# Seven-product blocks: running sums in two PSUM banks, four ScalarE copies and one 512-column VectorE addition instead of one copy and five additions

## The reference

```python
def hybrid_layer(x, ...):
    h = rms_norm(x, norm1_g)
    q, k, v, iq, ik, iw, a, c, g = split(h @ w_in, IN_SPLITS)
    # sparse attention on q, k, v, iq, ik, iw; convolutions on a and c
    ...
    # gated outputs of the three branches, the product with w_o, and a
    # feed-forward part (w_up, a short convolution, w_down)
```

## Time and profile before

| | |
|---|---|
| time, median of 3 runs | 1971.0 us (1969.97 to 1972.1) |
| span of the profiled execution | 1967.1 us |
| median of the runs less that span | 3.9 us |
| PE busy | 1954.6 us, 99% of the span |
| PEld busy | 1848.6 us, 94% |
| DVE busy | 1194.6 us, 61% |
| POOL busy | 1119.2 us, 57% |
| ACT busy | 402.2 us, 20% |

### The profile page before, as it was taken

How to read it: one execution, slowest core, us unless ns; L and a number is a source line. 1 busy time by engine, 2 the same in 40 slices (tenths; PEclk the granted TensorE clock), 3 DMA queues, 4 the chain that set the end, 5 groups by cost and what they waited for, 6 DMA issues and landing times. The chain is left out here.

```text
span 1967.1 us, 37363 instructions
## 1 busy us (share of the span) xinstructions
PE 1954.6 (99%) x14834; PEld 1848.6 (94%) x14834; DVE 1194.6 (61%) x3033; ACT 402.2 (20%) x978; POOL 1119.2 (57%) x750
## 2 busy tenths in 40 slices
PE   9999999999999999999999999999999999999999
PEld 7788889999899999999999899999999999999998
DVE  4244535989978477524888987667713487554541
ACT  2241521111321222110111222222102025220000
POOL 1000038785176588758678155487776674448783
PEclk9999999999999999999999999999999999999999
DMA  5313445444444454445444343454444442445544
GB/s 212 134 43 132 150 151 179 160 164 139 149 144 143 156 174 167 171 148 172 168 159 168 121 162 131 150 172 172 167 164 161 136 147 97 140 150 172 172 161 140
DMA packets 44267, 299.76 MB, mean 152 GB/s; under 512 B 5440, under 2 KB 6592, under 8 KB 10176
## 3 DMA queue, kind: packets, MB, share of 16 engines
q1 hardware_dynamic: 42560, 295.42, 43.7%
q10 hardware_dynamic: 1536, 1.97, 0.3%
HBM read 294.35 MB, written 1.05 MB: 150 GB/s over the span
## 5 line engine op out<-in xcount | busy, mean ns | idle before, releaser
L712 PE MATMUL bank<-arena,ring 128*128 128x128 f32 (+2 forms) x3854 | 603.4, 310 | 1.2 <-ACT arena L1344 0.6
L712 PEld LDWEIGHTS bank<-arena,ring 128*128 128x128 f32 x3854 | 540.4, 191 | 43.6 <-ACT arena L1344 3.1
L712 PE MATMUL bank<-xn,ring 128*128 128x128 f32 (+3 forms) x3104 | 467.8, 306 | 0.0
L712 PEld LDWEIGHTS bank<-xn,ring 128*128 128x128 f32 (+1 forms) x3104 | 424.4, 191 | 31.1 <-issue 4.4
L712 PE MATMUL bank<-arena 128*128 128x128 f32 (+3 forms) x3048 | 391.5, 284 | 0.0
L712 PEld LDWEIGHTS bank<-arena 128*128 128x128 f32 (+1 forms) x3048 | 364.9, 192 | 9.3 <-issue 1.5
L712 PE MATMUL bank<-arena,h_res 128*128 128x128 f32 x2696 | 322.4, 276 | 2.1 <-POOL h_res L1802 1.2
L712 PEld LDWEIGHTS bank<-arena,h_res 128*128 128x128 f32 x2696 | 310.6, 192 | 5.1 <-POOL h_res L1802 2.4
L1798 POOL TENSOR_TENSOR arena<-ring 128x1024 f32<-128x1024 f32 (+1 forms) x103 | 243.0, 2360 | 124.7 <-DMA ring<-wstream 124.2
L1798 POOL TENSOR_TENSOR h_res<-ring 128x1024 f32<-128x1024 f32 (+1 forms) x95 | 221.7, 2334 | 127.1 <-DMA ring<-wstream 111.9
L1849 DVE SCALAR_TENSOR_TENSOR bank<-arena,par,bank 128x256 f32<-128x256 f32 x640 | 259.5, 483 | 15.3 <-DVE arena L2265 7.7
(11 more groups left out here) (241 smaller groups left out, 1805.0 us busy)
## 6 DMA issues: line engine op xcount, KB each, us to landing
ring<-wstream SPq DMA_DIRECT2D x264, 1024.0 KB, 4.8
ring<-wstream SPq DMA_DIRECT2D x16, 768.0 KB, 4.2
cst<-consts SPq DMA_DIRECT2D x1, 2488.0 KB, 14.7
h_res<-tokens SPq DMA_DIRECT2D x2, 544.0 KB, 5.1
arena<-arena ACTq DMA_DIRECT2D x16, 64.0 KB, 3.4
out<-arena SPq DMA_DIRECT2D x4, 256.0 KB, 5.4
arena<-arena ACTq DMA_DIRECT2D x28, 32.0 KB, 3.1
ring<-wstream SPq DMA_DIRECT2D x2, 288.0 KB, 2.9
```

The lines of the kernel that those rows point to most:

```text
L712: return pe.matmul(o, lhs, rhs, start=start, stop=stop, skip_group_check=True)
```

## The change

The 179 fast blocks other than `down` and the first `attn` become `chain_block`. Products now add up in PSUM: P6 onto P1 and P7 onto both, P3 onto P5. Since a partial sum is wanted in several outputs, ACT copies it at four moments (`snapshot` 1, 5, 2 and 3), and the next product onto the same columns waits for the copy. Both banks of the block are taken at its start. The order of the products is P1, P2, P5, P6, P4, P3, P7; P3, the last that reads the ring, is the sixth and signals `slot_done`. DVE adds the 512 columns of both banks and the 512 copied ones in one instruction. `mix` takes the order t1, t2, t4, t3 in first blocks, and SP waits for `spent` (the last of the four) in place of `mixed`. On ACT other work is placed between the copies. `down` and the first `attn` blocks keep their form.

```diff
+    def take_pair(self, key):
+
+        self.turn["main"] += self.turn["main"] % 2
+        x = self.take("main", (key, "x"))
+        first, y = self.before, x + 1
+        self.turn["main"] += 1
+        self.counts.banks[key, "y"] = (y, 0, 0, 1, None)
+        second = self.freed_with.pop(y, (y, self.count[f"use{y}"]))
+        self.freed_with[y] = (x, self.count[f"use{x}"])
+        return {"x": x, "y": y}, [(self.sems[f"bank_free{b}"], n) for b, n in (first, second)]
...
                     sp.wait_ge(sems[f"slot_done{slot}"], n)
                     if held[slot]:
-                        sp.wait_ge(*e.at(("mixed", held[slot])))
+                        sp.wait_ge(*e.at(("spent", held[slot])))
...
 
+            def chain_block(block, plain, sums, ready=None, token_major=False):
+
+                slot = e.next_block()
+                w = ring[:, slot, :].rearrange("p (s k c) -> p s k c", s=4, c=P)
+                m = mixed_of(block).rearrange("p (s k c) -> p s k c", s=4, c=P)
+
+                def product(place, weight, act, opens=False):
+                    half, col = part_at[place]
+                    for k in range(4):
+                        one, two = (act(k), weight[:, k, :]) if token_major else (weight[:, k, :], act(k))
+                        ins = mm(bank[half], slice(0, P), slice(col, col + P), one, two, opens and k == 0, k == 3)
+                    return ins
+
+                pe.wait_ge(*e.landed(slot))
+                bank, emptied = e.take_pair(block)
+                for when in emptied:
+                    pe.wait_ge(*when)
+                for event in ready or ():
+                    pe.wait_ge(*e.at(event))
+                product("c22", w[:, 0], lambda k: plain(0, k, 0), opens=True).then_inc(*e.done("main_done", ("pe", (block, "p1"))))
+                product("c11", w[:, 3], lambda k: plain(1, k, 0), opens=True)
+                pe.wait_ge(*e.at((sums, "sum", 0)))
+                pe.wait_ge(*e.at(("mix1", block)))
+                product("c12", m[:, 0], lambda k: sums_at_k(sums, 0, k)).then_inc(*e.done("main_done", ("pe", (block, "p5"))))
+                pe.wait_ge(*e.at((block, "s1")))
+                pe.wait_ge(*e.at((sums, "sum", 1)))
+                pe.wait_ge(*e.at(("mix2", block)))
+                product("c22", m[:, 2], lambda k: sums_at_k(sums, 1, k))
+                pe.wait_ge(*e.at(("mixed", block)))
+                product("c21", m[:, 3], lambda k: plain(1, k, 1)).then_inc(*e.done("main_done", ("pe", (block, "p4"))))
+                pe.wait_ge(*e.at((block, "s5")))
+                pe.wait_ge(*e.at((sums, "sum", 3)))
+                product("c12", w[:, 2], lambda k: sums_at_k(sums, 3, k)).then_inc(*e.done(f"slot_done{slot}"))
+                pe.wait_ge(*e.at((block, "s2")))
+                pe.wait_ge(*e.at((sums, "sum", 2)))
+                pe.wait_ge(*e.at(("mix1b", block)))
+                product("c22", m[:, 1], lambda k: sums_at_k(sums, 2, k)).then_inc(*e.done("main_done", ("pe", (block, "t"))))
+
             def late_block(block, plain, sums, ready):
...
@@ -1449,14 +1518,18 @@
                     act.activation(p_, p_, ACT.Exp, scale=q_scale[:, 8 * t + h:8 * t + h + 1], bias=small[:, k:k + 1],
                                           accum_out=small[:, k + 4:k + 5]).then_inc(*e.step((L + "e", h, t)))
 
-            def heads(L, pr, pts, out, gates=None, beside=None):
+            def heads(L, pr, pts, out, block_of, meanwhile=None, beside=None):
                 for h in range(9):
                     if h < 8:
+                        snapshot(block_of(h), 1)
+                        snapshot(block_of(h), 5)
                         softmax(L, h, pr)
+                        snapshot(block_of(h), 2)
+                        if meanwhile:
+                            meanwhile(h)
+                        snapshot(block_of(h), 3)
...
@@ -1469,9 +1542,28 @@
 
             def first_product(key):
 
+                if snap_before(key):
+                    act.wait_ge(*e.at((snap_before(key), "c22")))
                 act.wait_ge(*e.at(("pe", (key, "x"))))
-                b = e.bank_of((key, "x"))
-                act.activation(p1c[:, b // 2 % 2, :], psum[b][:, 0:P], ACT.Copy).then_inc(*e.step((key, "p1")))
+                act.activation(snap(key)[:, 0:P], psum[e.bank_of((key, "x"))][:, 0:P], ACT.Copy).then_inc(*e.step((key, "p1")))
+
+            def snapshot(key, n):
+
+                done, of, to = {1: ("p1", "c22", "c11"), 5: ("p5", "c12", "c22"), 2: ("p4", "c22", "c12"), 3: ("t", "c22", "c21")}[n]
+                (half, col), at = part_at[of], snap_at[to]
+                if n == 1 and snap_before(key):
+                    act.wait_ge(*e.at((snap_before(key), "c22")))
+                act.wait_ge(*e.at(("pe", (key, done))))
+                act.activation(snap(key)[:, at:at + P], psum[e.bank_of((key, half))][:, col:col + P],
+                               ACT.Copy).then_inc(*e.step((key, f"s{n}")))
+
+            def snapshots(key, *meanwhile):
+
+                for n in (1, 5, 2):
+                    snapshot(key, n)
+                for work in meanwhile:
+                    work()
+                snapshot(key, 3)
 
             for l in range(2):
...
@@ -1789,7 +1900,18 @@
                     pool.wait_ge(*e.at(((block[0], "up" if block[1] == "up" else "x"), "sum", 2)))
                 if before_in_home(block):
                     pool.wait_ge(*e.at(("pe", (before_in_home(block), "t"))))
-                if block[2:] == (0, 0) and block[1] in ("a", "g", "conf", "attn", "o", "up", "mqk", "ret"):
+                if block[2:] == (0, 0) and block[1] in ("a", "g", "conf", "o", "up", "mqk", "ret"):
+                    t1, t3, t2, t4 = (m[:, size * c:size * c + size] for c in range(4))
+                    w11, w12, w22, w21 = (w[:, size * c:size * c + size] for c in range(4))
+                    pool.tensor_tensor(out=t1, in0=w12, in1=w11, op=ALU.subtract).then_inc(*e.step(("mix1", block)))
+                    pool.wait_ge(*e.at(("mix1", block)))
+                    pool.tensor_tensor(out=t2, in0=w22, in1=t1, op=ALU.subtract).then_inc(*e.step(("mix2", block)))
+                    pool.wait_ge(*e.at(("mix2", block)))
+                    pool.tensor_tensor(out=t4, in0=w21, in1=t2, op=ALU.subtract).then_inc(*e.step(("mixed", block)))
...
@@ -2244,13 +2367,24 @@
                     for event in [(stage, "y", q, t) for q in range(2) for t in range(2)]:
                         dve.wait_ge(*e.at(event))
 
-            def unite(key, out, cols, *after, token_major=False):
-
-                view = out[:, :, cols:cols + S].rearrange("p t (n c) -> p n t c" if token_major else "p n (t c) -> p n t c", c=P)
+            def unite(key, out, cols, *after):
+
                 for event in after:
                     dve.wait_ge(*e.at(event))
+                if len(key) == 4 and chained(key):
+                    dve.wait_ge(*e.at((key, "s3")))
+                    by = "p t (n c) -> p n t c" if key[1] in ("v", "mv", "rv") else "p n (t c) -> p n t c"
+                    x = e.bank_of((key, "x"))
+                    both = banks[:, 512 * x:512 * x + 1024].rearrange("p (t z) -> p t z", t=2)[:, :, 0:2 * P]
+                    dve.tensor_tensor(out[:, :, cols:cols + S].rearrange(by, c=P), both.rearrange("p t (n c) -> p n t c", c=P),
+                                      snap(key).rearrange("p (n t c) -> p n t c", n=2, t=2),
+                                      ALU.add).then_inc(*e.frees((key, "x"), (key, "c11")))
+                    e.counts.events[key, "c12"] = e.counts.events[key, "c22"] = e.counts.events[key, "c11"]
+                    dve.wait_ge(*e.at((key, "c11")))
+                    return
+                view = out[:, :, cols:cols + S].rearrange("p n (t c) -> p n t c", c=P)
                 x, y = psum[e.bank_of((key, "x"))], psum[e.bank_of((key, "y"))]
-                p1 = p1c[:, e.bank_of((key, "x")) // 2 % 2, :]
```

217 lines of the change are left out of this document (118 added, 99 removed).

## The result

The changed kernel takes 2008.8 us (median of 4 runs, 2007.2 to 2010.2) against 1970.5 (4 runs): 1.0195 times as long, 95% interval 1.0181 to 1.021. The prediction said 1991 us, with a range of 1976 to 2004. The kernel became slower, as forecast, but by 38.3 us where some 20 were forecast, and the time lies 4.8 us above the range.

What follows compares the result with a forecast made beforehand. The prediction took PE to bound the kernel. Its terms, 2.1 + 6.6 + 2.4 + 7.0 + 0.7 + 3.9 - 3.1 = 19.6 us, took the span from 1967.1 to 1986.7 and the median to 1991 us, range 1976 to 2004.

Steps and rivals of the forecast that it cites:

- What bounds the kernel: PE, busy 1954.6 of 1967.1 us; a change leaving its matmuls alone can give back at most 12.5 us.
- The ring's release: Chained blocks: slots released 2.68 us later, t4 complete at 2.97 and needed at 3.57; reserve falls from 5.07 to 0.60.
- Item 1: First blocks of `a`, `up` and `mqk`, six: three products now follow a late t4, 0.35 us each, +2.1 us.
- Item 2: `v` and first `iq` in L0 and L1, four blocks: fifth product waits for t4, +1.65 us each, +6.6.
- Item 3: Second blocks of `o` and C.ret, and six behind first blocks: t4 misses the fifth product, +2.4 us in all.
- Items 4 and 5: Late-landing transfers exceeding the reserve, 10 starts, +7.0 us; mixes slowed by DVE alone, five or so, +0.7 us.
- Waits for ACT: Copy 2 late in C's heads 4 to 7, 3.5 us, and copy 1 in L0.g's first block, 0.4; together +3.9 us.
- The failed step, first part: PE's waits for normalised probabilities and one for ACT: all credited as gain from fewer DVE additions, -3.1 us.
- The failed step, second part: In `heads`, ACT's queue ahead of copy 2, which has 0.4 us to spare; part of the +3.9 us for ACT.
- the weight path: Rival: it mostly keeps up, late landings are rare and ACT is in time; about 1980 us, chance 14%.
- ACT is no bound in common blocks: Rival claimed the opposite: ACT bounds everywhere, each of 179 blocks waits 0.2 us, +36, 2027 us; chance 8%.
- POOL's mixes did not shrink: Rival claimed they shrink without DVE beside them, so not slower, about 1968 us; 10% including waits and gains cancelling.
- the load is followed by the next activation at once: C's heads 4 to 7: assumed in the sum; rival had table switches hold ACT 1.28 us more each, 1996 us, 2%.

## Why the prediction was too low

- *What bounds the kernel*: right. 155 us less on DVE bought nothing.
- *The ring's release*: right in mechanism and size, t4 at 2.92 (2.97 forecast), issue at 5.55 (5.5).
- *Item 1, first blocks*: +2.1 forecast, +3.1 measured: each 0.43 to 0.56 instead of 0.35.
- *Item 2, `v` and `iq`*: +6.6 forecast, +6.9 measured.
- *Item 3*: +2.4 forecast, +2.1 measured. The six second blocks behind first ones lost nothing.
- *Items 4 and 5, late landings and slowed mixes*: +7.7 forecast, +4.9 measured, within the bounds of 2 to 12. The largest single one, 1.5 us in L0.up (4,0), came in another way: POOL held DVE's sums, and the next block, which now takes both its banks at its start, waited 1.05 us for the addition. Without it the forecast mechanism gave 3.4.
- *Waits for ACT*: +3.9 forecast; C's heads and L0.g gave 4.6. That the sum is near is in part luck. Heads 5 and 7 were close (0.7 and 0.5 forecast, 1.0 and 0.6 measured), but head 6 was 0.7 instead of 1.8, and head 4 was 2.0 instead of 0.5, and not by the table load.
- *The failed step, first part*: "I give the change all of these: -3.1 us". I took the waits for the probabilities as waits for a busy DVE, which fewer additions would shorten. In the first head they are waits for a DVE that POOL holds: the pair of L2146 spans 2.32 us beside POOL's subtraction of 1024 columns, 0.53 elsewhere. (And 1.0 of the 3.1 was put down to ACT, which got more work.) Nothing was gained, and `conf`, `sc` and `attn` lost 7.8 us. Of these 6.3 are the first heads: POOL's new order of four subtractions leaves DVE no gap. I had counted that order only as an earlier t4. The run with the old order there brought them back. The forecast also took PE's clock as full throughout: 3.4 of the 6.3 are the two stretches at 0.50 behind the long waits. In the other heads the runs point to the shift of the mixes: the late release alone, in the kernel before, costs 6.5 us by the medians, of which cut subtractions return 3.5.
- *The failed step, second part*: "Queued ahead of it in `heads` are now copies 1 and 5 and the exponentials" costs only what stands ahead of copy 2. I never asked what stands behind copy 3, the one that can't be made before the block's end. The boundary behind the last block of `o` does, and lost 10.7 us. The run that reorders ACT's work there gave 7.7 back.
- *Rivals*: the weight path did not keep up better than forecast, and ACT is no bound in common blocks, which start 6.25 us apart; POOL's mixes did not shrink (352.94 to 357.99, 5.05 us); the load is followed by the next activation at once (669.10 + 1.28, then 670.39).

These two parts make 10.7 + 7.8 + 3.1 = 21.6 us, nearly the whole difference of 21.3 between the 40.9 in the span and the 19.6 of the sum; the errors of the other terms and the smaller blocks cancel to within 0.3. The range failed with them: it was built from the spread of the terms that I had, with no room for one that was missing.

What stays open is a part of C's heads 4 and 5: the late release alone made each 1.2 us longer in the kernel before, out of 2.0 and 1.0 here, but no run took POOL's mix out of their way, since cut pieces hold DVE one after the other there.

## What to carry to other kernels

When work moves to an in-order engine, look at both sides of each new instruction: what stands ahead of it, and above all what stands behind the one that waits longest. When a change shifts when GpSimd runs, look for what VectorE does at the new time: here two-input operations stopped for up to the whole of a GpSimd subtraction (2.3 us), independent subtractions in a row left them no gap, and VectorE, idle for 48% of the span, was still the late one. A wait that costs PE 2 us can also cost it the clock behind, so count the stretches at half clock before you compare two times that differ by a few us. A term for relief ("the waits on that engine go") needs the reason for the wait, not its name in a list.
